# Overflow products of the large experts in three blocks in place of six

## The reference

```python
def moe_ffn(h, router_w, router_b, w_gu, b_gu, w_dn, b_dn):
    logits = (xf @ router_w + router_b).astype(jnp.float32)
    top_vals, top_idx = lax.top_k(logits, TOP_K)              # 4 of 32 experts per token
    gates = jax.nn.softmax(top_vals, axis=-1)
    ...
    def expert_block(args):
        xb, e = args
        gu = xb @ w_gu[e] + b_gu[e]                           # 1024 -> 2 x 1024
        glu = jnp.minimum(gu[:, :EXPERT_DIM], SWIGLU_LIMIT)
        lin = jnp.clip(gu[:, EXPERT_DIM:], -SWIGLU_LIMIT, SWIGLU_LIMIT)
        act = glu * jax.nn.sigmoid(SWIGLU_ALPHA * glu) * (lin + 1.0)
        return act @ w_dn[e] + b_dn[e]                        # 1024 -> 1024
```

## Time and profile before

| | us |
|---|---|
| median of 3 runs | 2346.53 |
| lowest and highest | 2342.76, 2346.98 |
| the profiled execution | 2342.93 |
| its span, first to last instruction | 2341.1 |
| TensorE busy | 2165.4 (92%) |
| VectorE busy | 1834.0 (78%) |
| ScalarE busy | 1366.4 (58%) |

### The profile page before, as it was taken

How to read it: one execution, slowest core, us unless ns; L and a number is a source line. 1 busy time by engine, 2 the same in 40 slices (tenths; PEclk the granted TensorE clock), 3 DMA queues, 4 the chain that set the end, 5 groups by cost and what they waited for, 6 DMA issues and landing times.

```text
span 2341.1 us, 41559 instructions
## 1 busy us (share of the span) xinstructions
PE 2165.4 (92%) x15487; PEld 1731.2 (74%) x15487; DVE 1834.0 (78%) x2152; ACT 1366.4 (58%) x1545; POOL 552.2 (24%) x434
## 2 busy tenths in 40 slices
PE   6899999867899399999999999999999999999994
PEld 5667888755678377778778778778778778778773
DVE  3699999948733777877877877877877877877885
ACT  4542223865742457667667667667667667667665
POOL 1007786764000102112112112112112112112110
PEclk8779999967999699999999999999999999999997
DMA  5011211020023279889889889889889889889896
GB/s 142 19 46 37 55 45 54 24 75 35 1 84 126 96 267 340 310 290 346 309 287 348 309 285 348 312 285 351 310 282 349 310 285 348 312 286 344 315 374 256
DMA packets 253598, 526.46 MB, mean 225 GB/s; under 512 B 33048, under 2 KB 59800, under 8 KB 253180
## 3 DMA queue, kind: packets, MB, share of 16 engines
q1 hardware_dynamic: 240268, 483.27, 57.6%
q0 software_dynamic: 13264, 42.34, 7.5%
HBM read 490.96 MB, written 35.91 MB: 225 GB/s over the span
## 4 chain that ended last, share of the span: by engine, by line
PE 70%; DMA 10%; DVE 8%; ACT 4%; issue 4%; POOL 2%; SPq 0%; DVEq 0%; ACTq 0%; POOLq 0%
PE ps L1754 13%; PE ps L1756 12%; PE ps L1755 12%; DMA e_raw<-in_w_gate_up_dram 9%; PE ps L1761 9%; PE ps L1429 5%; PE ps L1430 5%; PE ps L1431 5%; DVE e_wlo L2253 2%; PE ps L1766 1%; PE ps L1504 1%; PE ps L1634 1%; PE ps L1645 1%; PE ps L1584 1%; DVE a_s L2031 1%
## 5 line engine op out<-in xcount | busy, mean ns | idle before, releaser
L1312 ACT ACTIVATE e_whi<-e_raw 128x2048 fp32r<-128x2048 f32 x411 | 786.2, 1918 | 421.3 <-PE ps L1756 309.0
L2253 DVE TENSOR_TENSOR e_wlo<-e_raw,e_whi 128x2048 fp32r<-128x2048 f32 x410 | 926.8, 2286 | 66.3 <-ACT e_whi L1312 64.8
L1754 PE MATMUL ps<-e_whi,xh 128*128 128x512 f32 x1088 | 434.7, 400 | 0.0
L1755 PE MATMUL ps<-e_whi,xl 128*128 128x512 f32 x1088 | 424.3, 390 | 0.0
L1756 PE MATMUL ps<-e_wlo,xh 128*128 128x512 f32 x1088 | 424.1, 390 | 0.0
L941 POOL DMA_INDIRECT x_d<-ym,scur x34 | 70.6, 2078 | 871.0 <-ACT ym L1345 850.8
L1754 PEld LDWEIGHTS ps<-e_whi,xh 128*128 128x128 f32 x1088 | 204.3, 188 | 52.7 <-issue 12.9
L1756 PEld LDWEIGHTS ps<-e_wlo,xh 128*128 128x128 f32 x1088 | 204.3, 188 | 43.9
L1755 PEld LDWEIGHTS ps<-e_whi,xl 128*128 128x128 f32 x1088 | 204.5, 188 | 39.4
L1754 PE MATMUL ps<-e_whi,ath 128*128 128x512 f32 x544 | 221.7, 408 | 12.9 <-DVE atl L2281 12.9
L1756 PE MATMUL ps<-e_wlo,ath 128*128 128x512 f32 x544 | 213.3, 392 | 0.0
(11 more groups left out here) (351 smaller groups left out, 3345.1 us busy)
## 6 DMA issues: line engine op xcount, KB each, us to landing
e_raw<-in_w_gate_up_dram SPq DMA_DIRECT2D x275, 1024.0 KB, 5.2
e_raw<-in_w_down_dram SPq DMA_DIRECT2D x136, 1024.0 KB, 11.4
w_raw<-in_w_in_dram SPq DMA_DIRECT2D x20, 512.0 KB, 3.8
xt<-in_x_dram SPq DMA_DIRECT2D x8, 512.0 KB, 6.2
xr<-in_x_dram SPq DMA_DIRECT2D x8, 512.0 KB, 4.2
x_d<-x SPq DMA_DIRECT2D x8, 512.0 KB, 2.6
h_d<-h SPq DMA_DIRECT2D x8, 512.0 KB, 2.9
x<-x_d SPq DMA_DIRECT2D x8, 512.0 KB, 7.4
```

Of the source, the lines that this page charges most:

```text
L1312: nc.scalar.activation(e_whi[:, m % HRING, :], e_raw[:, m % RING, :], ACT.Copy).then_inc(s.e_hi, 1)
L1754: nc.tensor.matmul(dst, a_hi, slot_hi, start=False, stop=False, skip_group_check=True)
L1755: nc.tensor.matmul(dst, a_lo, slot_hi, start=False, stop=False, skip_group_check=True)
L2253: nc.vector.tensor_tensor(e_wlo[:, m % HRING, :], e_raw[:, m % RING, :], e_whi[:, m % HRING, :].bitcast(F32), ALU.subtract).then_inc(s.e_l ...
```

## The change

The six blocks become three. Gate and up of one half of the columns are computed together, ahead of the main matmuls of step 2 and of step 6, out of four raw pieces; the whole down projection's overflow is computed ahead of step 10, out of four raw pieces. Each block's last matmul counts up a new semaphore, `p_ov`. The two older pieces of each block (0 and 1, 4 and 5, 8 and 9) must stay in the ring until the block is done, so the loads that replace them wait for `p_ov` in place of `p_pc`. The clamps `go_out` and `ao_out` wait for `p_ov` too, and `go_out` moves back: behind `x_lo` in the first half, behind the low part of piece 8 in the second.

```diff
@@ -326,6 +326,7 @@
         self.e_xl = sem("e_xl")
         self.ld_xo = sem("ld_xo")
         self.p_xo = sem("p_xo")
+        self.p_ov = sem("p_ov")
         self.e_yo = sem("e_yo")
         self.e_over = sem("e_over")
         self.e_xoh = sem("e_xoh")
@@ -706,7 +707,10 @@
             def load(u, m, e):
 
                 before = u.kind if m >= RING else {"L": "S", "S": "L", "X": "X"}[u.kind]
-                if before == "L":
+                gone = (m + RING) % PIECES
+                if before == "L" and gone % 4 < 2:
+                    sp.wait_ge(s.p_ov, Unit(u.loop, 1, 0, "L").nth(3, gone // 4 + 1))
+                elif before == "L":
                     sp.wait_ge(s.p_pc, u.nth(PIECES, m + 1))
                 else:
                     sp.wait_ge(s.e_lo, u.nth(PIECES, m + 1))
@@ -1781,17 +1785,19 @@
                     pe.wait_ge(s.e_act, u.nth(8, 4 * j + (6 if g else 5)))
                     bias_into(ps[:, g, :], sel[:], D * g + 512 * j)
                 high(u, p)
-                if u.kind == "L" and half == 0:
-                    if p == 0:
+                if u.kind == "L" and p % 4 == 2:
+                    if j == 0:
                         pe.wait_ge(s.e_xoh, v.nth(1, 1))
                         pe.wait_ge(s.e_yo, v.nth(1, 1))
-                    if j == 1:
-                        pe.wait_ge(s.e_over, v.nth(8, 8 + (2 if g else 1)))
+                    else:
+                        pe.wait_ge(s.e_over, v.nth(8, 8 + 2))
                     high(u, p + 1)
-                    in_groups(2 + g, P, selo[:], bias.bitcast(F32)[:, D * g + 512 * j:D * g + 512 * j + 512], True, False)
-                    for k in range(KC):
-                        raw = gu_piece(e_raw, (p + k // 4) % RING)
-                        in_groups(2 + g, P, xo[:, k, :], raw[:, k % 4, :], False, k == KC - 1)
+                    for b in range(2):
+                        in_groups(2 + b, P, selo[:], bias.bitcast(F32)[:, D * b + 512 * j:D * b + 512 * j + 512], True, False)
+                        for k in range(KC):
+                            raw = gu_piece(e_raw, (4 * j + 2 * b + k // 4) % RING)
+                            o = in_groups(2 + b, P, xo[:, k, :], raw[:, k % 4, :], False, k == KC - 1)
+                    o.then_inc(s.p_ov, 1)
                 low(u, p)
                 hi_, lo_ = gu_piece(e_whi, p % HRING), gu_piece(e_wlo, p % HRING)
                 for c in range(4):
@@ -1816,16 +1822,15 @@
                     for b in range(2):
                         bias_into(ps[:, 4 + b, :], sel[:], 2 * D + 512 * b)
                 high(u, p)
-                if u.kind == "L" and q % 2 == 0:
-                    if q == 0:
-                        pe.wait_ge(s.e_over, v.nth(8, 8 + 5))
-                    pe.wait_ge(s.e_aoh, v.nth(2, q // 2 + 1))
+                if u.kind == "L" and q == 2:
+                    pe.wait_ge(s.e_over, v.nth(8, 8 + 5))
+                    pe.wait_ge(s.e_aoh, v.nth(2, 2))
                     high(u, p + 1)
-                    if q == 0:
-                        in_groups(2, D // GROUPS, selo[:], bias.bitcast(F32)[:, 2 * D:3 * D], True, False)
-                    for c in range(4):
-                        raw = dn_piece(e_raw, (p + c // 2) % RING)
-                        in_groups(2, D // GROUPS, ato[:, 2 * q + c, :], raw[:, c % 2, :], False, 2 * q + c == KC - 1)
+                    in_groups(2, D // GROUPS, selo[:], bias.bitcast(F32)[:, 2 * D:3 * D], True, False)
+                    for k in range(KC):
+                        raw = dn_piece(e_raw, (8 + k // 2) % RING)
+                        o = in_groups(2, D // GROUPS, ato[:, k, :], raw[:, k % 2, :], False, k == KC - 1)
+                    o.then_inc(s.p_ov, 1)
                 if q % 2 == 0:
                     pe.wait_ge(s.e_al, u.nth(2, q // 2 + 1))
                 low(u, p)
@@ -2283,11 +2288,11 @@
 
             def go_out(u, v, j):
 
-                dve.wait_ge(s.p_pc, u.nth(PIECES, 4 * j + 2 + RING))
+                dve.wait_ge(s.p_ov, v.nth(3, j + 1))
                 nc.vector.tensor_scalar(go[:], ps[:, 2, 0:P], LIMIT, None, ALU.min).then_inc(s.e_over, 1)
 
             def ao_out(u, v, j):
-                dve.wait_ge(s.p_pc, u.nth(PIECES, 4 * j + 4 + RING))
+                dve.wait_ge(s.p_ov, v.nth(3, j + 1))
                 nc.vector.tensor_scalar(uo[:], ps[:, 3, 0:P], LIMIT, -LIMIT, ALU.min, ALU.max).then_inc(s.e_over, 1)
                 dve.wait_ge(s.e_over, v.nth(8, 8 + 4 * j + 2))
                 nc.vector.scalar_tensor_tensor(out=uo[:], in0=uo[:], scalar=1.0, in1=go[:], op0=ALU.add, op1=ALU.mult).then_inc(s.e_over, 1)
@@ -2321,9 +2326,9 @@
                 lo(u, 2)
                 lo(u, 3)
                 g_out(u, 0)
-                go_out(u, v, 0)
                 lo(u, 4)
                 x_lo(u)
+                go_out(u, v, 0)
                 lo(u, 5)
                 a_out(u, 0)
                 ao_out(u, v, 0)
@@ -2331,8 +2336,8 @@
                 lo(u, 7)
                 at_lo(u, 0)
                 g_out(u, 1)
+                lo(u, 8)
                 go_out(u, v, 1)
-                lo(u, 8)
                 lo(u, 9)
                 a_out(u, 1)
                 ao_out(u, v, 1)
```

## The result

| | before | after |
|---|---|---|
| median | 2346.76 us (4 runs) | 2430.19 us (4 runs) |
| range | 2342.76 to 2347.16 | 2428.19 to 2431.41 |
| profiled execution | 2342.93 | 2431.41 |

What follows compares the result with a forecast made beforehand. Two nearly touching limits per pair of experts: TensorE in the large unit (L), the weight stream in the small (S). 6.4 us plus 1.6 clock loss, 8.0 a pair, 16 pairs: 128 on 2342.9, 2471 us; range 2395 to 2540.

Steps and rivals of the forecast that it cites:

- L6 issued: Load of the large unit's 1 MB weight piece 6, held for the first merged block: issue at 10.5 us, before 5.61.
- stall 1: TensorE idle ahead of step 5 of the large unit, waiting for the low part of its piece 5: 2.8 us.
- stall 2: TensorE idle ahead of the merged down block, waiting for ScalarE's copies of the second activations: 1.3 to 2.0 us.
- block 3: The merged down block ahead of step 10 of the large unit, forecast to end at 47.9 to 48.6 us.
- Parts 2 and 3: Held slots delay loads and stall the large unit, then weight loads back up in the small unit; pair +6.4 us, merging gain included.
- The backlog: Small unit's weight loads pile up after block 3; the next large unit's first piece lands 36.2 to 37.3 us after it.
- no stall in S: Rival: large-unit stalls come but the small unit's stream keeps up; +2.9 us a pair, 2389 or 2415 us; 14%.
- the clock falls at every stall: Rival: three clock losses of 1.6 us per pair, 11.2 us a pair in all, 2522 us; 20%.
- faster: Rival: the load queue catches up and only the merging gain is left, 2332 us; 4%.
- Two signs: Signs to look for: a pair of 93 to 96 us, and TensorE idle before the down block for 1.3 to 2.0.
- Part 4: TensorE's clock in the loop: one loss of 1.6 us per pair after the new stalls; the ends none and three.
- Part 1: Merged blocks save three entries and exits of 0.23 us per large unit: 0.7 us, 11 us in 16.

Runs made afterwards that it cites:

- e4: The changed kernel with ScalarE's copy of x in the large unit moved ahead of the split of piece 6; 2391.69 us, ratio 1.0193.
- e8: The changed kernel with ScalarE's x copy and both units' second-activation copies moved ahead of late weight splits; 2347.98 us, ratio 1.0005.
- e3: The kernel before with only the down projection's overflow merged into one block ahead of step 10; 2376.66 us, ratio 1.0127.
- e1: The kernel before with its six blocks, only the loads made to wait as in the change; 2401.33 us, ratio 1.0231.
- e6: e5 with the small unit's second-activation copy also moved ahead of the split of the next large unit's first piece; 2330.45 us, ratio 0.9928.
- e5: e2 with the large unit's copy of x moved ahead of the split of piece 6; 2341.86 us, ratio 0.9981 against the kernel before.
- e7: The kernel before with only the small unit's second-activation copy moved ahead of the next large unit's first split; 2339.12 us, ratio 0.9961.
- e2: The changed kernel with only gate and up merged, the down blocks two again and their loads as before; 2395.27 us, ratio 1.0211.

## Why the prediction was right, and where it was off

The forecast was slower, 2471 us, with a range of 2395 to 2540; measured were 2430. Point by point, in us from the start of the large unit:

| step of the prediction | predicted | profile after |
|---|---|---|
| L6 issued | 10.5 | 10.3 (1316.94) |
| stall 1, ahead of step 5 | 2.8 | 2.45 |
| stall 2, ahead of the down block | 1.3 to 2.0 | 1.04 |
| block 3 ends | 47.9 to 48.6 | 47.3 |
| next L0 lands after block 3 | 36.2 to 37.3 | 36.0 (1376.87 + 13.00) |
| stall at step 10 of the small unit | about 2 | 1.88 |
| pair | 93.0 to 94.8 | 92.16 |
| three pieces, S2 to S5 | 7.5 to 8.6 | 8.1 (1367.35 - 1359.21) |
| seven pieces, S5 to the next L0 | 23.1 | 22.6 (L0 in at 1389.87, S5 0.1 before its split) |
| clock losses in 16 pairs | 16 | 6, after some 48 stalls |

**Parts 2 and 3 hold.** The chain split of L6, copy of x, low parts, step 5 was shown by e4, which cut it on ScalarE and got 38.5 us back. Stall 2 went in e8 with `at_hi` and `at_over` moved ahead of the split of S0. The backlog was shown by e3. That the held slots cost by themselves was shown by e1, and that the long gate and up blocks do not by e6. The rival "no stall in S" is out by the 1.88 us of the profile, "the clock falls at every stall" by its six dips, and "faster" by the sign; but the part of it that I had dismissed is true of another kernel: with the copy of x ahead of the split, being 4.9 us late with L6 costs nothing (e5, e6). Two signs were set too high: the pair is 92.16 us, not 93 to 96, and the stall ahead of the down block 1.04, not 1.3 to 2.0.

**Part 4 was the mis-sized term.** I took one clock loss of 1.6 us per pair, 26 us. A dip costs 1.7 us as read from the clock, near enough; but only six of them lie in the loop, against none in the kernel before, 10 us. Five of the six fall in the first three pairs, one in the other thirteen; no working of mine had that, and one per pair was a guess between none and three. That is 16 us too much in a forecast of +128 against +88 in the profile. The other part is the pair: +6.4 predicted, +4.6 measured, some 29 us over 16 pairs. Taken against the middles, block 3 ends 0.95 us sooner (stall 1 0.35, stall 2 0.6), and L0 lands 0.75 sooner behind it: S2 is in after 5.2 us in place of 5.56, and the seven pieces up to L0 take 22.6 us in place of 23.1. The three pieces between them took 8.1 us, 2.7 each, which is inside the range. Against these 45 us stand 6 that I had not counted: the first three pairs are 9.7, 6.3 and 8.7 us over their counterparts, which is 2 us more than the pair's own 4.6 and the five dips among them, and 4 us lie outside the loop.

**The skill's rule** on the clock (the Trainium skill, TensorE: Matmul & The Clock Gate, "HAM oscillation — how this bites in real kernels"), which the prediction read so that each of these stalls would pay, does not describe them: six of some 48 did. The page's own example waits some 3 to 5 us for its DMA in each tile, longer than the 0.8 to 2.7 us of these 48, so the prediction stretched it. In e1 two pairs of three did pay, after stalls of some 1.86 us.

**Part 1** was sized low: e6 against e7 gives 0.70 us a pair for two merges, where I had 0.46.

## What to carry to other kernels

When a change lets a resource be held longer, do not ask only whether the load behind it is still in time for its consumer; look at what stands behind that consumer in its engine's fixed order, for that is what comes late (here x_hi behind a split, at a cost of 39 us that one moved line took away). Where one stage keeps the DMA engines full, transfers that the stage before it leaves undone come on top there, even if the engines idle before (1.5 us a pair in e3); how much of that TensorE sees hangs on the order too (about 1 us in e8). And a merge that saves entries and exits is worth having only where it holds nothing that the fuller stage needs: gate and up merged gave 0.7 us a pair (less 5 us once, in the first), down merged took 1 to 1.5.

## What the runs showed of the hardware that I had not expected

The length of an idle stretch does not say whether the clock falls. In the changed kernel a stall of 2.45 us was followed by the 2.4 GHz level in the pair shown, and so were most; in e1 a stall of 1.86 us was followed by 1.2 GHz, and one of 1.84 us a pair earlier was not. In e1 a dip comes in two pairs of three through the loop, eleven in all. e3 has a stall of the same length at the same place in each pair (1.82 to 1.98 us) and three dips. e2, with fewer stalls than the change, had nine against six. So a loop with a stall of 2 us per round may pay for its clock in most rounds or in few; what in the timing decides was not tested.
